# Four modulation pairs of each first FFN dealt out over the last unit, the passage into the mix and the mix's weight remainders

## The reference

```
c_act = silu(c)
for l in range(2):
    mod = c_act @ w_ada[l] + b_ada[l]                      # 1024 -> 9 * 1024
    sh1, sc1, g1, sh2, sc2, g2, sh3, sc3, g3 = split(mod, 9)
    x = x + 0.5 * g1 * swiglu(modulate(x, sh1, sc1), ffn1...)
    x = x + g2 * token_mix(modulate(x, sh2, sc2), ...)     # begins with u @ w_in[l]
    x = x + 0.5 * g3 * swiglu(modulate(x, sh3, sc3), ffn2...)
...
def modulate(x, shift, scale):
    return rms_norm(x) * (1 + scale) + shift
def swiglu(u, w_gate, w_up, w_down):
    return (silu(u @ w_gate) * (u @ w_up)) @ w_down
```

## Time and profile before

| | |
|---|---|
| median of 3 runs | 1766.36 us (1764.45 to 1766.58) |
| the profiled execution, its own time | 1763.35 us |
| its span | 1761.7 us |
| TensorE matmul busy | 1688.8 us, 96% |
| VectorE busy | 1361.5 us, 77% |
| ScalarE busy | 981.9 us, 56% |
| mean granted clock of TensorE | 0.992 |

### The profile page before, as it was taken

How to read it: one execution, slowest core, us unless ns; L and a number is a source line. 1 busy time by engine, 2 the same in 40 slices (tenths; PEclk the granted TensorE clock), 3 DMA queues, 4 the chain that set the end, 5 groups by cost and what they waited for, 6 DMA issues and landing times.

```text
span 1761.7 us, 24830 instructions
## 1 busy us (share of the span) xinstructions
PE 1688.8 (96%) x8511; PEld 1391.1 (79%) x8518; DVE 1361.5 (77%) x2106; ACT 981.9 (56%) x1540; POOL 46.8 (3%) x92
## 2 busy tenths in 40 slices
PE   6999989999999999999889999999999989999998
PEld 4888877888788878888778887788787876888886
DVE  7887777767776678777687587877868579999997
ACT  4444554665544464446447555444645657777775
POOL 0000000000000000000000000000000000000000
PEclk9999999999999999999999999999999999999999
DMA  9898853225677748886623248987483535999994
GB/s 368 338 348 320 332 194 141 87 98 194 237 292 260 259 175 325 315 314 260 239 76 114 99 167 307 350 326 292 169 309 118 205 132 197 378 355 353 370 354 164
DMA packets 61802, 437.42 MB, mean 248 GB/s; under 512 B 6816, under 2 KB 7328, under 8 KB 9504
## 3 DMA queue, kind: packets, MB, share of 16 engines
q1 hardware_dynamic: 47360, 338.44, 50.9%
q0 software_dynamic: 12672, 92.28, 14.2%
q10 hardware_dynamic: 1696, 5.72, 0.9%
HBM read 435.36 MB, written 1.05 MB: 248 GB/s over the span
## 4 chain that ended last, share of the span: by engine, by line
PE 78%; DVE 11%; DMA 5%; ACT 3%; issue 3%; SPq 0%; DVEq 0%; ACTq 0%; POOLq 0%
PE bank L2043 23%; PE bank L2045 22%; PE bank L2044 22%; DVE w_lo L1085 3%; DVE ada_w L1117 2%; DMA raw<-weight_stream 2%; PE bank L2342 2%; DMA ada_w<-ada_pairs 1%; PE bank L2360 1%; DMA arena<-ada_pairs 1%; ACT w_hi L531 1%; PE bank L2172 1%; PE bank L2322 1%; PE bank L2080 1%; DVE arena L1174 1%
## 5 line engine op out<-in xcount | busy, mean ns | idle before, releaser
L2043 PE MATMUL bank<-w_hi,uT_hi 128*128 128x512 f32 (+1 forms) x1384 | 543.1, 392 | 26.6 <-DVE w_lo L1085 11.0
L531 ACT ACTIVATE w_hi<-raw 128x1024 fp32r<-128x1024 f32 x396 | 396.6, 1053 | 292.8 <-PE bank L2045 263.4
L1085 DVE TENSOR_TENSOR w_lo<-raw,w_hi 128x1024 fp32r<-128x1024 f32 x388 | 457.0, 1221 | 129.2 <-ACT w_hi L531 128.0
L2044 PE MATMUL bank<-w_lo,uT_hi 128*128 128x512 f32 (+1 forms) x1384 | 530.0, 383 | 0.0
L2045 PE MATMUL bank<-w_hi,uT_lo 128*128 128x512 f32 (+1 forms) x1384 | 529.6, 383 | 0.0
L2043 PEld LDWEIGHTS bank<-w_hi,uT_hi 128*128 128x128 f32 x1384 | 262.8, 190 | 84.6 <-issue 17.7
L2045 PEld LDWEIGHTS bank<-w_hi,uT_lo 128*128 128x128 f32 x1384 | 262.5, 190 | 50.9
L2044 PEld LDWEIGHTS bank<-w_lo,uT_hi 128*128 128x128 f32 x1384 | 263.4, 190 | 45.5
L1117 DVE CUSTOM_DVE_ANT_0 ada_w<-ada_w,cmpw 128x1024 f32<-128x1024 f32 x176 | 207.3, 1221 | 12.8 <-DMA ada_w<-ada_pairs 12.8
L2043 PE MATMUL bank<-w_hi,r_arena 128*128 128x512 f32 (+1 forms) x392 | 155.9, 398 | 4.2 <-DVE r_arena L1940 2.5
L2045 PE MATMUL bank<-w_hi,r_arena 128*128 128x512 f32 (+1 forms) x392 | 152.0, 388 | 0.0
(11 more groups left out here) (376 smaller groups left out, 1962.5 us busy)
## 6 DMA issues: line engine op xcount, KB each, us to landing
raw<-weight_stream SPq DMA_DIRECT2D x216, 1024.0 KB, 5.6
ada_w<-ada_pairs POOLq DMA_DIRECT2D x88, 1024.0 KB, 5.2
raw<-expert_blocks SPq DMA_DIRECT2D x48, 1024.0 KB, 4.9
ada_w<-expert_blocks SPq DMA_DIRECT2D x32, 1024.0 KB, 5.0
cmpw<-expert_blocks SPq DMA_DIRECT2D x16, 1024.0 KB, 5.0
arena<-ada_pairs SPq DMA_DIRECT2D x5, 1024.0 KB, 13.4
ada_w<-ada_pairs SPq DMA_DIRECT2D x3, 1024.0 KB, 13.4
cmpw<-compress_w ACTq DMA_DIRECT2D x2, 1024.0 KB, 14.0
```

The source lines that it names most:

```text
L531: act.activation(w_hi[:, b], v, ACT.Copy).then_inc(hi_done, 1)
L1085: V.tensor_tensor(w_lo[:, b], v, f32(w_hi[:, b]), ALU.subtract).then_inc(split_done, 1)
L2043: pe.matmul(dst, xh, hi, start=first, stop=False, skip_group_check=True)
L2044: pe.matmul(dst, xh, lo, start=False, stop=False, skip_group_check=True)
```

## The change

The loop over pairs 20 to 23 behind the remainders of u_mix+1 goes. `late_stage_pair(l, j)` does one of them, and each stands alone in VectorE's program: pair 20 in the last unit of the first FFN, between the first half of the hidden product and the first split; pair 21 behind `norm_behind_ffn`; pair 22 where all four were; pair 23 between the remainders of block 0 and block 1 of u_mix+2. `last_unit` takes two functions more, `first` and `second`; only `first` is used, and only by the first FFN. The programs of TensorE, ScalarE, SyncE and GpSimd keep their text. GpSimd's loads move in time, since each waits for a pair.

```diff
-            def last_unit(u, f):
+            def last_unit(u, f, first=lambda: None, second=lambda: None):
                 extra_block(u, 2)
                 hidden(f, (0,))
+                first()
                 split(u + 1, (0,))
                 h_tile(0, (hL_hi_done, f // FFN_UNITS + 1), hL_ready)
                 hidden(f, (1,))
+                second()
                 split(u + 1, (1,))
...
+            def late_stage_pair(l, j):
+                ada_pair(pair_place(l, "ffn1", j), mods[:, 2 * j - 8:2 * j - 6])
...
-                last_unit(u0 + n - 1, f0 + n - 1)
+                last_unit(u0 + n - 1, f0 + n - 1, lambda: late_stage_pair(l, 20))
                 norm_behind_ffn(stage, stage + 1, stage + 1, (extra_used, stage + 1), lambda i: split_half(u0 + n, 2, i))
+                late_stage_pair(l, 21)
...
                 split(u_mix + 1, (2,))
-                for j in range(20, 24):
-                    ada_pair(pair_place(l, "ffn1", j), mods[:, 2 * j - 8:2 * j - 6])
+                late_stage_pair(l, 22)
...
-                split(u_mix + 2, (0, 1))
+                split(u_mix + 2, (0,))
+                late_stage_pair(l, 23)
+                split(u_mix + 2, (1,))
```

## The result

| | before | changed |
|---|---|---|
| median of the runs | 1765.98 us (1764.45 to 1766.58, 4 runs) | 1749.71 us (1746.26 to 1753.85, 4 runs) |
| profiled execution, its own time | 1763.35 us | 1749.12 us |
| its span | 1761.7 us | 1747.4 us |
| its mean granted clock | 0.992 | 0.995 |

The ratio is 0.9917, with a 95% interval from 0.9894 to 0.9939. The profiled execution is 14.2 us shorter in its own time and 14.3 in its span; the forecast was 14.0. The median of 1749.71 lies 2.7 us under the forecast of 1752.4 and inside the range. One of the 18 runs of the kernel before in the second set of experiments took 2423.82 us at a granted clock of 0.651; no ratio uses it.

The account below looks back on a forecast made before the run. TensorE was held bound between u_mix+1 and u_mix+2 by pairs ahead of the remainders' chain. Waits 9.44 plus slow starts 4.53, say 14.0 us, take 1763.35 to 1749.4; the median 3.0 above gives 1752.4, range 1748.5 to 1758.0.

Parts of the forecast that it names:

- The bound: Between u_mix+1 and u_mix+2, TensorE's waits for weight remainders, 4.52 and 4.92 us, go wholly; nothing replaces them.
- Pair 22: Alone ahead of the means, done by 246.2; first remainder of u_mix+2 at 249.2, block 0 done at 251.5.
- Pair 23: Between remainders of u_mix+2, 251.5 to 253.9; holds block 1's up by 0.8 us only, done about 256.2.
- Pairs 20 and 21: In VectorE's gaps in the last unit and behind the norm: cost 0 to 0.2 us a layer and 0.
- The load at 206: Pair 22's earlier load in the dense stretch delays ScalarE's weight block by 0, range 0 to 2.8 us a layer.
- The clock: Without the wait between u_mix+1 and u_mix+2, slow starts of the 48 matmuls go: 1.64 + 2.89 = 4.53 us.
- The first: Rival in the passage: earlier transfer delays the weight block 1.8 us a layer, 3.5 comes back: 1755.9; chance 0.14.
- The second: Rival in the mix: waits go, slow starts stay or turn up elsewhere, only 9.4 us gained: 1757.0; chance 0.07.
- The third: Rival at a later handover: VectorE late for the next unit, half the gain returns, gain 7: 1759.4; chance 0.04.
- The fourth: Slower rival in the last unit: pair 20 not landed, passage late one for one; 10 us late gives 1772.4; chance 0.03.
- The size: Whole kernel: waits 9.44 plus slow starts 4.53 give 13.97, say 14.0 us, off the profiled execution.

Follow-up runs that it names:

- second set of experiments: Four experiment kernels run beside the kernel before on the same chip, which had a median of 1762.63 us (18 runs); the changed kernel was run again.
- kernel with a warm seam: Kernel before, plus 20 TensorE matmuls on zeros in the wait between u_mix+1 and u_mix+2 in each layer: 1760.16 us, ratio 0.9974.
- held load: Changed kernel, with GpSimd's load of pair 22 held back until the norm (about 231.7 instead of 206.1): 1750.79 us, ratio 0.9933.
- second pair in the last unit: Changed kernel, with pair 21 moved from behind the norm into the last unit, right behind pair 20: 1755.7 us, ratio 0.9969.
- first set of experiments: Four experiment kernels run beside the kernel before on the same chip, which had a median of 1764.37 us (19 runs); the changed kernel was run again.
- kernel with pair 23 alone: Kernel before, with only pair 23 moved between the remainders of blocks 0 and 1 of u_mix+2; 20, 21, 22 stay: 1753.58 us, ratio 0.9944.

## Why the prediction was right

*The bound.* The seam's wait was what the two long waits for remainders were; both are gone (4.52 and 4.92), and nothing took their place: the row behind the gate has no idle time in either layer.

*Pair 22.* The first remainder was put at 249.2 and the end of block 0 at 251.5; the rows have 249.17 and 251.45. The 3.0 us from the last pair to that remainder, carried over whole, held because the road by way of ScalarE's root, table load and rounding is the same.

*Pair 23.* Put at 251.5 to 253.9, it stands at 251.45 to 253.74, and the remainders behind it are done at 256.1 (said 256.2). The statement that TensorE wants block 1 only in the second half of its matmuls was not needed. What the prediction did not see is that this move is idle: with 22 and 23 both ahead of the means, the first remainder at 252.09 is early enough as well.

*Pairs 20 and 21.* The cost taken as 0 of a range to 0.2 was 0.01 at the last unit in layer 0 (205.70 to 205.71). Behind the norm the next remainder moved by 0.05 (234.83 to 234.88), and not for the pair: it is over at 234.1, and the remainder waits 0.82 more for ScalarE.

*The load at 206.* Taken as 0 of a range to 2.8 a layer. The number held, the reason given for it did not. The prediction said that a load which comes late to full queues leaves the older one little to lose. But in the kernel before, the load of pair 21 (issued at 197.57) had 38.0% of the traffic between 200 and 206 us and the stream 23.0%. What saved the block wanted at 209.6 is when the bytes come: GpSimd's queue moves the first bytes of the load issued at 206.08 between 209.5 and 210 us, when that block has just landed (209.59). That is a margin of under 1 us, so this term was in part luck, and two of the six executions with the early load show a wait longer by 0.4 and 1.0 us. By the Trainium skill, "DMA: Bandwidth & Descriptors", section "Queues, rings and completion order", each DMA engine goes round-robin over the queues that have work. The trace agrees with it from 210 us on (40.7% for GpSimd's queue, 46.3% for the stream) and shows no sharing with this load in the 3.5 us ahead of that. Whether its descriptors were ready by then no row shows.

*The clock.* Taken as 4.53. The kernel with a warm seam has the two units 4.2 us shorter for it alone; in the changed kernel the 48 matmuls are 1.55 and 2.80 us shorter, 4.35 in all.

*The rivals.* The first, at its price, is answered by the held load; a smaller price in some executions is not excluded. The second, that the slow starts turn up elsewhere, is half right in what is seen: the profiled execution of the changed kernel has a stretch at half clock at 1359 that the one before has not. But the one before has two at 918 and 983 that the changed one has not, behind waits of 1.68 and 1.57 us that both kernels have. Of the two repeats of the changed kernel one has falls at 903, 1088, 1334 and 1344 and none at 1359, the other has one at 1359, half as long. No execution with a short or no wait at the seam has one there. So the falls elsewhere differ between executions of one kernel, and they nearly cancel in this pair. The third: no later handover is late. TensorE's waits behind the unit, for r_arena and for the arena, are 3.5 and 1.7 us in both traces, and the lead of 6.3 us that layer 0 gains at its seam is still 5.9 at 493 us. The fourth was made to happen on a small scale by the second pair in the last unit: there VectorE does wait for a transfer, 1.92 us, and everything behind it is late as the rival said. The changed kernel has no such wait.

*The size.* 14.3 us of span against 14.0. Behind the second seam the changed kernel leads by 13.9 us, which is the sum as predicted; what follows, falls of the clock on either side and one shorter wait, adds 3.5 and takes 3.1. Of the 2.7 us by which the median lies under the forecast, 2.4 come from one term that has nothing to do with the change: the median was put 3.0 above the profiled execution, as before, and lies 0.6 above it. The medians of before and changed kernel differ by 16.3, 15.2 and 10.6 us in the three sets, so how near the median came is in part luck; the terms each have their row.

## What to carry to other kernels

Work that nobody waits for soon costs what it stands in front of, not what it takes: look for the item in the engine's own order that heads a chain through other engines, and keep the filler behind it, in gaps that the timeline shows as idle. Price a wait of TensorE with the slow start behind it, and remember that the last part of a wait can be worth less than the first. Move until the wait is gone and stop there: here two pairs of four brought the whole gain, and a second pair in a gap for one cost 3.7 us by the medians and 6.0 by the spans. That one wait does not grow does not show an earlier transfer to be free: look at the blocks that land next, and at more than one execution.

## What the runs showed that I had not expected

I had taken a fall of TensorE's clock as something that follows long waits. It also comes without one (in the changed kernel no wait of over 0.3 us stands in the 20 us ahead of the fall at 1359), and not at the same places in each execution. The changed kernel, its first profiled execution, by stretches (the third number from the end is the granted clock):

```profile
905.00:907.00 2.00, 2.00 (x10) 1.67 (x9) 1.74 (x3) 2.00 (x7) 0.00 (x0) 1.00 0.01 4
1359.00:1363.00 4.00, 4.00 (x11) 3.13 (x11) 3.87 (x7) 2.89 (x4) 0.00 (x0) 0.50 0.00 0
```

The same kernel, the execution of the first set of experiments:

```profile
905.00:907.00 2.00, 2.00 (x6) 1.51 (x5) 1.58 (x2) 2.00 (x5) 0.00 (x0) 0.54 0.00 0
1359.00:1363.00 4.00, 4.00 (x32) 3.65 (x30) 1.28 (x3) 3.03 (x5) 0.00 (x0) 1.00 0.60 180
```

What TensorE did just before was the same. Its timeline in the first of these executions, clock up behind it, and then in the second, clock down:

```profile
902.91 1.14 PE L2329 MATMUL bank<-arena 64*128 64x256 f32 x8 [1.68 <-DVE arena L1477]
903.98 0.50 PE L2050 MATMUL bank<-w_hi,uT_hi 128*128 128x512 f32 x1
904.31 0.39 PE L2051 MATMUL bank<-w_lo,uT_hi 128*128 128x512 f32 x1
```

```profile
902.24 1.14 PE L2329 MATMUL bank<-arena 64*128 64x256 f32 x8 [1.69 <-DVE arena L1477]
903.31 0.70 PE L2050 MATMUL bank<-w_hi,uT_hi 128*128 128x512 f32 x1
903.81 0.63 PE L2051 MATMUL bank<-w_lo,uT_hi 128*128 128x512 f32 x1
```

A wait of 1.69 us with many small matmuls around it drops the clock in one execution and one of 1.68 does not in another; the 1.54 at the seam of the kernel with pair 23 alone did not; the four of 2.9 to 4.9 shown above all did. What a fall costs can be read by setting the start of each matmul in the changed execution beside the same matmul before: the lead is 13.9 us behind the seam of layer 1, 15.5 behind 918 and 17.1 behind 983, where only the execution before has a fall, 17.4 ahead of 1359 and 14.3 behind it, where only the changed one has. That is 1.6 us for a short fall and some 3 for a long one. Waits vary too: TensorE's wait at L2179 near 1087 us is 2.26, 3.71 and 1.49 us in the three profiled executions of the changed kernel, and the 3.71 has a fall behind it that the other two have not. A few more or fewer of these are the size of the spread in the runs (1746.26 to 1753.85), and a difference of under 4 us between two single profiles of this kernel says nothing until they are counted. What decides it in a given execution no run here shows.
